# Another order for the mixer's tasks on four engines of one core, in a two-layer Hyena, MLA and GLA encoder

## The chip, the cores and the metric

The kernel runs on one core of one Trainium2 chip. Its time is the device time of one launch, in microseconds. The engines, each with its own queue of instructions, are TensorE (PE), VectorE (DVE), ScalarE (ACT), GpSimd (POOL) and SyncE (SP), which here issues transfers only.

## What is computed

A two-layer encoder on 256 rows of 1024 numbers, all in float32. Each layer is a half-weighted gated FFN, a mixer and a second half-weighted FFN, each on RMS-normed input and added to x:

```python
def hybrid_layer(x, ...):
    x = x + 0.5 * swiglu_ffn(rms_norm(x, ffn1_norm), ...)
    proj = rms_norm(x, mix_norm) @ w_in          # split in ten parts
    y_hy = hyena_mixer(hy_in, ...)
    y_mla = mla_mixer(mla_cq, mla_ckv, mla_kr, ...)
    y_gla = gla_mixer(gla_q, gla_k, gla_v, gla_gf, gla_gb, gla_r, ...)
    x = x + jnp.concatenate([y_hy, y_mla, y_gla], axis=-1) @ w_out
    return x + 0.5 * swiglu_ffn(rms_norm(x, ffn2_norm), ...)
```

The mixer has three branches. **Hyena** convolves 768 columns with three taps, splits them in v, x1 and x2, and computes z = x1 * longconv(v), y = x2 * longconv(z), where a long convolution is a transform, a complex product with the filter's spectrum and an inverse transform; then an RMS norm. **MLA** is attention of four heads from normed low-rank latents (256 for queries, 128 for keys and values), with 64 rotated columns per head, softmax over 256 keys, an RMS norm. **GLA** is gated linear attention of four heads in both directions, with gates log_sigmoid(...)/16; an RMS norm per head, times silu(r).

## The kernel before

**Splitting.** A float32 matrix product is made of three passes of TensorE over operands split in a high and a low part (`passes`, L921 to L925): high by high, high by low, low by high. Weights come as 1 MB slots through a ring of three buffers. SP fetches slot n when DVE has made the low part of slot n - 3 (L250 to L256); ACT makes the high part (`hi`, L372, w_high) once TensorE has used slot n - 3; DVE the low part (`lo`, L606, w_low); TensorE then uses it and counts `s_used`. Slots go in a fixed order: 33 of an FFN, the mixer's 15 (S_G3, S_G2, S_G1, S_G4 of two slots each for w_in; S_UQN, S_UQR, S_UKV for the latents; S_WO to S_WO+3 for w_out), 33 of the second FFN from FFN2 on. `Fori` runs the layer's body twice.

**The order in the mixer** is written out by hand, one list of calls per engine, tied by semaphores ("marks"). An engine does its list strictly in order, so an instruction that waits holds all that follow it. The parts that matter here:

- *Gates.* TensorE L1146 makes the gate logits after S_G1; DVE adds the bias (L825); ACT does Abs, Exp, Ln (L533 to L535); DVE makes the level exponents (L830 to L832).
- *Short convolution.* ACT writes the centre tap (`conv_centre`, L454), DVE adds the other two (`taps`, L697, L699), TensorE transposes (`turn_conv`, L1097), ACT copies out (`natural`, L457).
- *Long convolution* o (0 or 1): TensorE transforms (`hy_dft`, L1057); ACT copies the odd half (`spectrum_odd`); DVE's `products` adds and subtracts (L749, L750), multiplies by the filter's spectrum (L759, L760), combines (L761, L762) and folds (L763, L764, mark h_y); TensorE inverts (`hy_inverse`, L1069); DVE multiplies by x1 or x2 (`gated`, L769). The Hyena norm is a square on ACT (L579), a small chain on POOL (`rstd`) and a scale on DVE (L874).
- *Queries and keys.* TensorE makes q without and with rotation (S_UQN, S_UQR), then the first keys, values, second keys (S_UKV, L1181 on). DVE multiplies the rotated part by cosine and sine (L851 to L853, mark a_qt), POOL adds (L349, mark a_qr; L344 is the same for the keys), TensorE transposes (L1198), ACT copies the result (QR). ACT copies also QN, KN and VM from PSUM.
- *GLA levels* b = 0 to 7: ACT's `level_exp` (L480, into silu_gate), DVE's `level_qk` (L706), TensorE's `level_scores` (L1050), DVE's `level_keep` (L716, a masked copy; mark g_la). POOL's `levels` (L319, four adds) prepares the exponents of the next level. Level scores use PSUM banks 0 to 3 one after the other, so level b + 1 on TensorE waits for the keep of level b.
- *Attention* in two halves of 128 rows: `scores` (L1075, L1076), `score_max` (L721), `probs` (L489), `turn_probs` (L1083), `probs_turned`, `attend` (L1090), `attended` (L730).
- *Output.* `turn_group` (L930) transposes the three branches' outputs in four groups, `turned_high` and `turned_low` (L614) split them, `project` multiplies by w_out in quarters; L1245 is the GLA output. Then `update` (L646) and the next norm (L940).

For the change's own places, the list of TensorE around the first inverse is:

```python
keys((0, 1))
for t in range(T):
    e.wait_ge(g_vr.sem, g_vr.at(l, t + 1))
    passes(PS[:, 5 + t, :], KVH..., WH[p][:, 1, :], WL[p][:, 1, :], True, True)
e.wait_ge(h_pr.sem, h_pr.at(l, 1))
keys((2, 3)).then_inc(s_used.sem, 1)
hy_inverse(l, 0, 0).then_inc(h_inv.sem, 1)
e.wait_ge(a_qr.sem, a_qr.at(l))
```

## Time and profile before

| | us |
|---|---|
| median of 3 runs (1086.48 to 1090.4) | 1088.77 |
| the profiled execution, whole | 1088.98 |
| its span in the profile | 1087.2 |
| TensorE busy in the span | 1035.0 |
| DVE, ACT, POOL busy | 607.5, 493.0, 104.5 |
| mixer of layer 1, first conv transposes to the next norm | 259.1 to 350.4 |
| mixer of layer 2, the same | 793.4 to 886.1 |

Times in the rows are counted from the start of the span. A row of the waits says which line waited for which, how long in all, how often, and the longest. A row of the timeline gives start and duration in us, engine, line, instruction, operands and shapes, how many were merged, and in brackets the idle time of the engine before it and what ended it. PEclk is the clock granted to TensorE as a share of 2.4 GHz. Ends of matmuls are modelled, so one can overlap the next by a few tenths of a microsecond.

### The profile page before, as it was taken

The numbers are of one execution on the slowest core, as the hardware profiler recorded it, in microseconds if no ns is written. First come the engines' busy times: TensorE is split into PE (matmuls) and PEld (weight loads), VectorE is DVE, ScalarE is ACT, GpSimd is POOL, SyncE is SP. The second block draws the span as 40 slices with busy tenths as digits, with TensorE's granted clock in tenths as the row PEclk, the third lists the DMA queues.
The fourth block names the chain that finished last, engine by engine and source line by source line (L and its number), as shares of the span: only waits on it lengthen the run. The fifth ranks groups of instructions, "written<-read, shape, count | busy, mean of one in ns | idle before, by whom it ended". The sixth has DMA issues, their size and how long they took to land.

```text
span 1087.2 us, 18043 instructions
## 1 busy us (share of the span) xinstructions
PE 1035.0 (95%) x7060; PEld 936.7 (86%) x7060; DVE 607.5 (56%) x650; ACT 493.0 (45%) x654; POOL 104.5 (10%) x159
## 2 busy tenths in 40 slices
PE   6999999998789999999999999999977999999996
PEld 6999999787468999999889999998865789999995
DVE  4644454756964645444565554457579455445544
ACT  6443344447444534444364344435565454433342
POOL 1000000331511000000010000005025110000000
PEclk9999999999889999999999999999997999999998
DMA  8554545245312455555445455544242026554551
GB/s 306 204 205 178 187 187 193 81 153 194 116 40 78 168 186 187 193 186 176 180 153 208 182 190 193 193 155 155 94 178 85 33 78 233 187 184 175 188 203 49
DMA packets 26117, 177.07 MB, mean 163 GB/s; under 512 B 3120, under 2 KB 3632, under 8 KB 5200
## 3 DMA queue, kind: packets, MB, share of 16 engines
q1 hardware_dynamic: 24912, 174.21, 44.0%
q0 software_dynamic: 720, 1.95, 0.7%
q8 instruction: 36, 0.59, 0.2%
q10 hardware_dynamic: 432, 0.18, 0.1%
q14 instruction: 17, 0.14, 0.0%
HBM read 175.63 MB, written 1.05 MB: 163 GB/s over the span
## 4 chain that ended last, share of the span: by engine, by line
issue 89%; POOL 9%; POOLq 0%; DMA 0%; DVE 0%; ACT 0%; DVEq 0%; SPq 0%
POOL mixer_scratch L319 4%; POOL mixer_scratch L340 1%; POOL mixer_scratch L339 1%; POOL statistics L296 1%; POOL statistics L306 0%; DMA x<-in_x_dram 0%; POOL x_normed L344 0%; POOLq L220 0%; POOL mixer_scratch L341 0%; POOL statistics L305 0%; POOL statistics L303 0%; DVE x_normed L913 0%; POOL x_normed L349 0%; POOL statistics L295 0%; POOL statistics L294 0%
## 5 line engine op out<-in xcount | busy, mean ns | idle before, releaser
L609 DVE TENSOR_TENSOR w_low<-w_raw,w_high 128x2048 fp32r<-128x2048 f32 x163 | 375.4, 2306 | 234.1 <-ACT w_high L378 234.1
L923 PE MATMUL psum<-xT_high,w_high 128*128 128x256 f32 x1536 | 437.0, 285 | 4.0 <-DVE xT_low L614 3.4
L925 PE MATMUL psum<-xT_high,w_low 128*128 128x256 f32 x1536 | 434.6, 283 | 0.0
L924 PE MATMUL psum<-xT_low,w_high 128*128 128x256 f32 x1536 | 434.6, 283 | 0.0
L378 ACT ACTIVATE w_high<-w_raw 128x2048 fp32r<-128x2048 f32 x163 | 311.2, 1915 | 119.6 <-PE psum L925 117.0
L923 PEld LDWEIGHTS psum<-xT_high,w_high 128*128 128x128 f32 x1536 | 294.6, 192 | 8.0 <-DVE xT_low L614 4.1
L924 PEld LDWEIGHTS psum<-xT_low,w_high 128*128 128x128 f32 x1536 | 294.6, 192 | 1.9 <-issue 0.5
L925 PEld LDWEIGHTS psum<-xT_high,w_low 128*128 128x128 f32 x1536 | 294.6, 192 | 0.0
L407 ACT ACTIVATE silu_gate<-psum 128x256 f32<-128x256 f32 x88 | 33.8, 384 | 273.0 <-PE psum L925 272.9
L923 PE MATMUL psum<-w_high,hT_high 128*128 128x512 f32 (+1 forms) x360 | 139.9, 389 | 0.0
L924 PE MATMUL psum<-w_low,hT_high 128*128 128x512 f32 (+1 forms) x360 | 139.7, 388 | 0.0
L925 PE MATMUL psum<-w_high,hT_low 128*128 128x512 f32 (+1 forms) x360 | 139.2, 387 | 0.0
L629 DVE TENSOR_TENSOR hidden<-silu_gate,psum 128x256 f32<-128x256 f32 x88 | 37.0, 421 | 123.4 <-ACT silu_gate L407 123.4
L925 PEld LDWEIGHTS psum<-w_high,hT_low 128*128 128x128 f32 x360 | 67.6, 188 | 14.1
L923 PEld LDWEIGHTS psum<-w_high,hT_high 128*128 128x128 f32 x360 | 67.8, 188 | 13.4 <-issue 0.8
L303 POOL TENSOR_TENSOR statistics<-statistics,constants 128x1 f32<-128x1 f32 x14 | 2.7, 190 | 789.6 <-ACT x_normed L385 789.6
L924 PEld LDWEIGHTS psum<-w_low,hT_high 128*128 128x128 f32 x360 | 67.8, 188 | 12.2
L923 PE MATMUL psum<-w_high,xT_high 128*128 128x512 f32 (+1 forms) x128 | 51.7, 404 | 0.0
L319 POOL TENSOR_TENSOR mixer_scratch<-mixer_scratch 128x128 f32<-128x128 f32 x56 | 41.5, 741 | 105.1 <-ACT silu_gate L480 101.8
L449 ACT ACTIVATE mixer_scratch<-psum 128x512 f32<-128x512 f32 (+4 forms) x52 | 29.0, 606 | 48.2 <-PE psum L1097 18.5
L924 PE MATMUL psum<-w_low,xT_high 128*128 128x512 f32 (+1 forms) x128 | 50.0, 391 | 0.0
L925 PE MATMUL psum<-w_high,xT_low 128*128 128x512 f32 (+1 forms) x128 | 49.9, 390 | 0.0
(166 smaller groups left out, 782.6 us busy)
## 6 DMA issues: line engine op xcount, KB each, us to landing
w_raw<-in_w_dram SPq DMA_DIRECT2D x163, 1024.0 KB, 4.8
...
```

Source lines behind the costliest of these rows:

```text
L296: e.tensor_tensor(b, b, cst[:, I_POW:I_POW + n], ALU.pow).then_inc(done.sem, 1)
L319: return e.tensor_tensor(to[:, :, side, :], to[:, :, side, :], o, ALU.add)
L339: link(l, e.tensor_tensor(HS[:, p, o * 256:(o + 1) * 256], a, b, ALU.add))
L340: link(l, e.tensor_tensor(HD[:, p, o * 256:(o + 1) * 256], a, b, ALU.subtract))
L378: e.activation(WH[p][:], raw[p][:], ACT.Copy).then_inc(s_hi.sem, 1)
L407: e.activation(sg[:, f, :], PS[:, 4 + 2 * pr + f, 0:SEQ], ACT.Silu).then_inc(s_silu.sem, 1)
L449: r = e.activation(dst, src, ACT.Copy, **kw)
L609: e.tensor_tensor(WL[p][:], raw[p][:], WH[p][:].bitcast(F32), ALU.subtract).then_inc(s_lo.sem, 1)
L629: e.tensor_tensor(hid[:, f, :], sg[:, f, :], PS[:, 4 + 2 * pr + f, SEQ:2 * SEQ], ALU.mult).then_inc(s_h.sem, 1)
L923: e.matmul(out, ah, bh, start=start, stop=False)
L924: e.matmul(out, ah, bl, start=False, stop=False)
L925: return e.matmul(out, al, bh, start=False, stop=stop)
```

## The change

No arithmetic changes; calls change their places in the lists, `products` is cut in `join`, `multiply`, `combine` and `fold`, and two marks are new: a_km is signalled by the first keys and a_vm by the values, so that ACT can copy them before all of S_UKV is used. Some waits move with the calls. By engine:

- POOL: levels(2) comes after the rotation add (L349) instead of before it; the Hyena `rstd` before levels 4 and 5.
- ACT: the high splits of S_G4 and S_G4+1 come earlier, those of S_WO+1 and S_WO+2 later; VG and RG are copied in two halves around `natural(3)` and the split of S_WO; the first keys' copy comes before the first levels; the level exponentials are spread out among the softmax and copies.
- DVE: S_G1+1 and S_G4+1 are split earlier, S_WO+1, S_WO+2 and S_WO+3 later; the first product is spread around the splits of S_UQR and S_UKV; the rotation of the queries and both products come before the levels 1 and 2.
- TensorE: the first transform comes before the rows of S_G4+1, the first inverse before the second keys, the second transform before the query transposes; heads of scores, levels and projection quarters are interleaved differently, and a quarter of the first projection group follows the GLA output.

The diff, with the indentation of the engines' bodies cut and no context lines:

```diff
@@ -202 +202 @@
-        a_kn, a_v = mark("k_copied", 2), mark("v_copied", 2)
+        a_km, a_vm, a_kn, a_v = mark("first_keys", 1), mark("values", 1), mark("k_copied", 2), mark("v_copied", 2)
@@ -347 +346,0 @@
-levels(l, 2)
@@ -349,0 +349 @@
+levels(l, 2)
@@ -350,0 +351 @@
+rstd(l, h_sq, 2, T_SH, T_RH, I_H, 2, h_r)
@@ -353 +353,0 @@
-rstd(l, h_sq, 2, T_SH, T_RH, I_H, 2, h_r)
@@ -515,0 +516,11 @@
+def values_out(t):
+    e.wait_ge(s_used.sem, used(l, S_G4 + 1))
+    copy(VG[:, t, :], PS[:, 5 + t, 0:256])
+    copy(RG[:, t, :], PS[:, 5 + t, 256:512], g_vr)
+def attended_squares(s):
+    e.wait_ge(a_oe.sem, a_oe.at(l, s + 1))
+    e.activation(TT[:, 2 * s:2 * s + 2, :].rearrange("p a b -> p (a b)"), xn[:, s, 256:768], ACT.Square,
+                 accum_out=st[:, T_SM + s:T_SM + s + 1]).then_inc(a_sq.sem, 1)
@@ -520,0 +532 @@
+hi(l, S_G4)
@@ -529,2 +541 @@
-natural(l, 1, 2, 4)
-hi(l, S_G4)
+hi(l, S_G4 + 1)
@@ -536 +546,0 @@
-hi(l, S_G4 + 1)
@@ -541,0 +552 @@
+natural(l, 1, 2, 4)
@@ -543 +554 @@
-natural(l, 3, 1, 4)
+spectrum_odd(l, 0, 1)
@@ -546,5 +556,0 @@
-e.wait_ge(s_used.sem, used(l, S_G4 + 1))
-for t in range(T):
-    copy(VG[:, t, :], PS[:, 5 + t, 0:256])
-    copy(RG[:, t, :], PS[:, 5 + t, 256:512], g_vr)
-spectrum_odd(l, 0, 1)
@@ -552 +558,2 @@
-level_exp(l, 1)
+values_out(0)
+natural(l, 3, 1, 4)
@@ -553,0 +561,4 @@
+values_out(1)
+e.wait_ge(a_km.sem, a_km.at(l))
+copy(KN[:, 0:2, :].rearrange("p a b -> p (a b)"), PS[:, 4, :], a_kn)
+level_exp(l, 1)
@@ -557,5 +568 @@
-level_exp(l, 2)
-hi(l, S_WO + 1)
-e.wait_ge(s_used.sem, used(l, S_UKV))
-copy(KN[:, 0:2, :].rearrange("p a b -> p (a b)"), PS[:, 4, :], a_kn)
-copy(KN[:, 2:4, :].rearrange("p a b -> p (a b)"), PS[:, 1, :], a_kn)
+e.wait_ge(a_vm.sem, a_vm.at(l))
@@ -564 +571 @@
-level_exp(l, 3)
+spectrum_odd(l, 1, 7)
@@ -568,2 +575,4 @@
-spectrum_odd(l, 1, 7)
-hi(l, S_WO + 2)
+hi(l, S_WO + 1)
+e.wait_ge(s_used.sem, used(l, S_UKV))
+copy(KN[:, 2:4, :].rearrange("p a b -> p (a b)"), PS[:, 1, :], a_kn)
+level_exp(l, 2)
@@ -572,5 +581,2 @@
-level_exp(l, 4)
-level_exp(l, 5)
-probs(l, 0)
-level_exp(l, 6)
-probs_turned(l, 0)
+hi(l, S_WO + 2)
+level_exp(l, 3)
@@ -580,2 +586,5 @@
-level_exp(l, 7)
-turned_high(l, 2, 0, Y_BANKS[0], Y_TILES[0], C_GO, by_parity)
+level_exp(l, 4)
+probs(l, 0)
+level_exp(l, 5)
+probs_turned(l, 0)
+level_exp(l, 6)
@@ -582,0 +592 @@
+turned_high(l, 2, 0, Y_BANKS[0], Y_TILES[0], C_GO, by_parity)
@@ -584,4 +594,3 @@
-for s in range(T):
-    e.wait_ge(a_oe.sem, a_oe.at(l, s + 1))
-    e.activation(TT[:, 2 * s:2 * s + 2, :].rearrange("p a b -> p (a b)"), xn[:, s, 256:768], ACT.Square,
-                 accum_out=st[:, T_SM + s:T_SM + s + 1]).then_inc(a_sq.sem, 1)
+level_exp(l, 7)
+attended_squares(0)
+attended_squares(1)
@@ -590,2 +599,2 @@
-for g in range(1, 3):
-    turned_high(l, 2, g, Y_BANKS[g], Y_TILES[g], C_GO)
+turned_high(l, 2, 1, Y_BANKS[1], Y_TILES[1], C_GO)
+turned_high(l, 2, 2, Y_BANKS[2], Y_TILES[2], C_GO)
@@ -741 +750 @@
-            def products(l, o, b):
+            def join(l, o, b):
@@ -751 +760,6 @@
-e.wait_ge(h_pr.sem, h_pr.at(l, o + 1))
+            def pairs(v):
+return v.rearrange("p (j c) n -> p j c n", c=2)
+            def multiply(l, o):
@@ -754,0 +769,11 @@
+e.wait_ge(h_pr.sem, h_pr.at(l, o + 1))
+e.tensor_tensor(pairs(Y), pairs(C), both(KA[:]), ALU.mult)
+link(l, e.tensor_tensor(pairs(TT), pairs(C), both(KI[:]), ALU.mult))
+            def combine(l):
+y, t = pairs(Y), pairs(TT)
+e.tensor_tensor(y[:, :, 0, :], y[:, :, 0, :], t[:, :, 1, :], ALU.subtract)
+link(l, e.tensor_tensor(y[:, :, 1, :], y[:, :, 1, :], t[:, :, 0, :], ALU.add))
+            def fold(l):
@@ -756,7 +780,0 @@
-def four(v):
-    return v.rearrange("p (j c) n -> p j c n", c=2)
-u, yy, tt = four(C), four(Y), four(TT)
-e.tensor_tensor(yy, u, both(KA[:]), ALU.mult)
-link(l, e.tensor_tensor(tt, u, both(KI[:]), ALU.mult))
-e.tensor_tensor(yy[:, :, 0, :], yy[:, :, 0, :], tt[:, :, 1, :], ALU.subtract)
-link(l, e.tensor_tensor(yy[:, :, 1, :], yy[:, :, 1, :], tt[:, :, 0, :], ALU.add))
@@ -767,0 +786,2 @@
+if o == 0:
+    e.wait_ge(c_nat.sem, c_nat.at(l, 3))
@@ -811,0 +832,2 @@
+lo(l, S_G1 + 1)
@@ -818,3 +839,0 @@
-e.wait_ge(q_hi.sem, q_hi.at(l, 2))
-e.scalar_tensor_tensor(out=KVL[:], in0=PS[:, 6, 0:SEQ], scalar=par[:, C_KVN:C_KVN + 1],
-                       in1=KVH[:].bitcast(F32), op0=ALU.mult, op1=ALU.subtract).then_inc(q_lo.sem, 1)
@@ -822 +841 @@
-lo(l, S_G1 + 1)
+e.memset(G[:, 2:4, :], 0.0)
@@ -828 +847,4 @@
-e.memset(G[:, 2:4, :], 0.0)
+e.wait_ge(q_hi.sem, q_hi.at(l, 2))
+e.scalar_tensor_tensor(out=KVL[:], in0=PS[:, 6, 0:SEQ], scalar=par[:, C_KVN:C_KVN + 1],
+                       in1=KVH[:].bitcast(F32), op0=ALU.mult, op1=ALU.subtract).then_inc(q_lo.sem, 1)
+lo(l, S_G4 + 1)
@@ -833 +854,0 @@
-lo(l, S_G4 + 1)
@@ -836,0 +858,2 @@
+join(l, 0, 0)
+multiply(l, 0)
@@ -840,3 +863,3 @@
-products(l, 0, 0)
-level_qk(l, 1)
-lo(l, S_WO)
+combine(l)
+fold(l)
@@ -854 +876,0 @@
-level_qk(l, 2)
@@ -856,4 +878,7 @@
-level_qk(l, 3)
-lo(l, S_WO + 1)
-e.wait_ge(a_qr.sem, a_qr.at(l))
-products(l, 1, 6)
+lo(l, S_WO)
+level_qk(l, 1)
+join(l, 1, 6)
+multiply(l, 1)
+combine(l)
+fold(l)
+level_qk(l, 2)
@@ -861 +886,2 @@
-level_qk(l, 4)
+gated(l, 1, 6)
+level_qk(l, 3)
@@ -864,7 +890 @@
-level_qk(l, 5)
-lo(l, S_WO + 2)
-level_keep(l, 2)
-gated(l, 1, 6)
-level_qk(l, 6)
-level_keep(l, 3)
-level_qk(l, 7)
+level_qk(l, 4)
@@ -876 +896,2 @@
-level_keep(l, 4)
+level_keep(l, 2)
+level_qk(l, 5)
@@ -878 +899 @@
-turned_low(l, 2, 0, Y_BANKS[0], Y_TILES[0], C_GO, by_parity)
+level_keep(l, 3)
@@ -879,0 +901,2 @@
+level_keep(l, 4)
+turned_low(l, 2, 0, Y_BANKS[0], Y_TILES[0], C_GO, by_parity)
@@ -880,0 +904 @@
+level_qk(l, 6)
@@ -881,0 +906 @@
+level_qk(l, 7)
@@ -887,0 +913 @@
+lo(l, S_WO + 1)
@@ -891,0 +918 @@
+lo(l, S_WO + 2)
@@ -899 +925,0 @@
-lo(l, S_WO + 3)
@@ -900,0 +927 @@
+lo(l, S_WO + 3)
@@ -1126 +1152,0 @@
-filter_dft(l, 1)
@@ -1129 +1154,0 @@
-e.wait_ge(q_kr.sem, q_kr.at(l))
@@ -1133,0 +1159,2 @@
+filter_dft(l, 1)
+e.wait_ge(q_kr.sem, q_kr.at(l))
@@ -1159 +1185,0 @@
-rows(l, 1, S_G4 + 1, 1, 512, (5, 6)).then_inc(s_used.sem, 1)
@@ -1161,0 +1188 @@
+rows(l, 1, S_G4 + 1, 1, 512, (5, 6)).then_inc(s_used.sem, 1)
@@ -1186 +1213 @@
-keys((0, 1))
+keys((0, 1)).then_inc(a_km.sem, 1)
@@ -1189,3 +1216,2 @@
-    passes(PS[:, 5 + t, :], KVH[:, t * P:(t + 1) * P], KVL[:, t * P:(t + 1) * P], WH[p][:, 1, :], WL[p][:, 1, :], True, True)
-e.wait_ge(h_pr.sem, h_pr.at(l, 1))
-keys((2, 3)).then_inc(s_used.sem, 1)
+    r = passes(PS[:, 5 + t, :], KVH[:, t * P:(t + 1) * P], KVL[:, t * P:(t + 1) * P], WH[p][:, 1, :], WL[p][:, 1, :], True, True)
+r.then_inc(a_vm.sem, 1)
@@ -1192,0 +1219,3 @@
+e.wait_ge(h_oc.sem, h_oc.at(l, 1))
+keys((2, 3)).then_inc(s_used.sem, 1)
+e.wait_ge(a_v.sem, a_v.at(l, 2))
@@ -1193,0 +1223,2 @@
+e.wait_ge(h_z.sem, h_z.at(l, 1))
+hy_dft(l, 1, 6)
@@ -1201,3 +1231,0 @@
-e.wait_ge(a_v.sem, a_v.at(l, 2))
-e.wait_ge(h_z.sem, h_z.at(l, 1))
-hy_dft(l, 1, 6)
@@ -1205 +1232,0 @@
-level_scores(l, -1)
@@ -1206,0 +1234,3 @@
+e.wait_ge(a_kn.sem, a_kn.at(l, 2))
+level_scores(l, -1)
+scores(l, 0, (2,))
@@ -1208 +1238,2 @@
-scores(l, 0, (2, 3)).then_inc(a_s.sem, 1)
+scores(l, 0, (3,)).then_inc(a_s.sem, 1)
+hy_inverse(l, 1, 6).then_inc(h_inv.sem, 1)
@@ -1210 +1241,2 @@
-hy_inverse(l, 1, 6, (0,))
+e.wait_ge(h_z.sem, h_z.at(l, 2))
+scores(l, 1, (0, 1, 2))
@@ -1212 +1243,0 @@
-hy_inverse(l, 1, 6, (1,)).then_inc(h_inv.sem, 1)
@@ -1213,0 +1245 @@
+scores(l, 1, (3,)).then_inc(a_s.sem, 1)
@@ -1215,5 +1247 @@
-e.wait_ge(h_z.sem, h_z.at(l, 2))
-scores(l, 1, (0, 1))
-level_scores(l, 4)
-scores(l, 1, (2, 3)).then_inc(a_s.sem, 1)
-e.wait_ge(a_pte.sem, a_pte.at(l, 1))
+attend(l, 0)
@@ -1222,2 +1250 @@
-attend(l, 0)
-level_scores(l, 5)
+level_scores(l, 4)
@@ -1224,0 +1252,2 @@
+level_scores(l, 5)
+attend(l, 1)
@@ -1229,2 +1257,0 @@
-attend(l, 1)
-project(l, 0, 0, 1)
@@ -1233 +1260 @@
-project(l, 0, 1, 0)
+project(l, 0, 0, 1)
@@ -1235 +1262 @@
-project(l, 0, 1, 1).then_inc(s_used.sem, 1)
+project(l, 0, 1, 0)
@@ -1247,0 +1275 @@
+project(l, 0, 1, 1).then_inc(s_used.sem, 1)
```

## Rows read from the trace of the kernel before

**Rows 1.** Page, part 1: busy time of each engine.
```profile
PE 1035.0 (95%) x7060; PEld 936.7 (86%) x7060; DVE 607.5 (56%) x650; ACT 493.0 (45%) x654; POOL 104.5 (10%) x159
```

**Rows 2.** Waits of TensorE, 251 to 351 us: total, times, longest.
```profile
PE psum L1069 <- DVE mixer_scratch L764: 3.4, 1, 3.4
PE psum L1050 <- DVE mixer_scratch L716: 3.0, 2, 2.0
PE psum L1097 <- DVE mixer_scratch L699: 2.7, 2, 1.7
PE psum L1198 <- POOL x_normed L349: 2.7, 1, 2.7
PE psum L1083 <- ACT mixer_scratch L489: 1.3, 1, 1.3
PE psum L930 <- DVE x_normed L874: 0.9, 1, 0.9
```

**Rows 3.** Windows, 275 to 310 us: PE, PEld, DVE, ACT, POOL busy, PEclk, DMA.
```profile
275.00:310.00 35.00, 25.86 (x156) 17.15 (x155) 30.81 (x34) 15.36 (x33) 15.65 (x22) 0.80 0.30 116
```

**Rows 4.** Timeline of TensorE: start, duration, line, shapes, count [wait before it].
```profile
244.38 1.13 PE L1146 MATMUL psum<-hidden,gate_weights 32*128 32x256 f32 x4
...
259.14 0.72 PE L1097 MATMUL psum<-constants,mixer_scratch 128*128 128x128 f32 x4 [1.74 <-DVE mixer_scratch L699]
...
268.46 0.47 PE L923 MATMUL psum<-hT_high,w_high 128*128 128x256 f32 x1
...
275.27 0.28 PE L923 MATMUL psum<-kvT_high,w_high 128*128 128x256 f32 x1
...
350.39 0.82 PE L940 MATMUL psum<-diag_rstd,x 128*128 128x128 f32 x5 [0.30 <-DVE diag_rstd L621]
...
793.43 0.72 PE L1097 MATMUL psum<-constants,mixer_scratch 128*128 128x128 f32 x4 [1.74 <-DVE mixer_scratch L699]
...
886.13 2.05 PE L940 MATMUL psum<-diag_rstd,x 128*128 128x128 f32 x16 [0.30 <-DVE diag_rstd L621]
```

**Rows 5.** Timeline of TensorE: eight 256-column passes, twice.
```profile
266.92 1.89 PE L1057 MATMUL psum<-mixer_scratch,dft 128*128 128x256 f32 x8
...
279.55 3.65 PE L1069 MATMUL psum<-mixer_scratch,inverse_dft 128*128 128x256 f32 x8 [3.40 <-DVE mixer_scratch L764]
```

**Rows 6.** Timeline of ACT: gate logarithm, copies of QR.
```profile
252.40 0.64 ACT L535 ACTIVATE mixer_scratch<-mixer_scratch 128x512 f32<-128x512 f32 x1
...
287.43 1.07 ACT L449 ACTIVATE mixer_scratch<-psum 64x512 f32<-64x512 f32 x2 [2.06 <-PE psum L1198]
```

**Rows 7.** Timeline of DVE: first taps; S_UKV's split; first and last operation of the second product.
```profile
257.08 0.48 DVE L697 SCALAR_TENSOR_TENSOR mixer_scratch<-psum,par,mixer_scratch 128x255 f32<-128x255 f32 x1
...
270.65 2.29 DVE L609 TENSOR_TENSOR w_low<-w_raw,w_high 128x2048 fp32r<-128x2048 f32 x1 [3.60 <-ACT w_high L378]
...
290.45 0.69 DVE L749 TENSOR_TENSOR mixer_scratch<-psum,mixer_scratch 128x512 f32<-128x512 f32 x1 [1.70 <-PE psum L1057]
...
296.52 0.90 DVE L764 TENSOR_TENSOR mixer_scratch<-mixer_scratch 128x512 f32<-128x512 f32 x1
```

**Rows 8.** Timeline of DVE and POOL: a split beside POOL's add; rotation adds, two levels.
```profile
227.35 2.29 DVE L609 TENSOR_TENSOR w_low<-w_raw,w_high 128x2048 fp32r<-128x2048 f32 x1
...
227.52 2.44 POOL L344 TENSOR_TENSOR x_normed<-mixer_scratch 128x128 f32<-128x128 f32 x1 [2.10 <-DVE mixer_scratch L809]
...
284.50 1.26 POOL L349 TENSOR_TENSOR x_normed<-mixer_scratch 128x512 f32<-128x512 f32 x1
...
285.73 4.31 POOL L319 TENSOR_TENSOR mixer_scratch<-mixer_scratch 128x128 f32<-128x128 f32 x4
...
300.02 1.86 POOL L319 TENSOR_TENSOR mixer_scratch<-mixer_scratch 128x128 f32<-128x128 f32 x4 [3.15 <-ACT silu_gate L480]
```

**Rows 9.** Page, parts 5 and 6: high splits on ACT; transfers of weights.
```profile
L378 ACT ACTIVATE w_high<-w_raw 128x2048 fp32r<-128x2048 f32 x163 | 311.2, 1915 | 119.6 <-PE psum L925 117.0
...
w_raw<-in_w_dram SPq DMA_DIRECT2D x163, 1024.0 KB, 4.8
```

More of the change, by code:

```diff
@@ L853, in _ @@
                 e.tensor_tensor(t2[:, :, :, 32:64], q[:, :, :, 0:32], rp(1, 32, 64), ALU.mult).then_inc(a_qt.sem, 1)
+                gated(l, 0, 0)
+                lo(l, S_WO)
[4 more added lines that the diff above has]
+                fold(l)
                 level_qk(l, 2)
-                gated(l, 0, 0)
+                level_keep(l, 0)
+                gated(l, 1, 6)
                 level_qk(l, 3)
-                lo(l, S_WO + 1)
-                e.wait_ge(a_qr.sem, a_qr.at(l))
-                products(l, 1, 6)
-                level_keep(l, 0)
-                level_qk(l, 4)
                 score_max(l, 0)
                 level_keep(l, 1)
-                level_qk(l, 5)
-                lo(l, S_WO + 2)
-                level_keep(l, 2)
-                gated(l, 1, 6)
-                level_qk(l, 6)
-                level_keep(l, 3)
-                level_qk(l, 7)
+                level_qk(l, 4)
                 e.wait_ge(h_r.sem, h_r.at(l))
@@ L875, in _ @@
                 r.then_inc(h_yy.sem, 1)
+                level_keep(l, 2)
+                level_qk(l, 5)
+                score_max(l, 1)
+                level_keep(l, 3)
+                attended(l, 0)
                 level_keep(l, 4)
-                score_max(l, 1)
                 turned_low(l, 2, 0, Y_BANKS[0], Y_TILES[0], C_GO, by_parity)
-                attended(l, 0)
                 level_keep(l, 5)
+                level_qk(l, 6)
                 attended(l, 1)
+                level_qk(l, 7)
                 level_keep(l, 6, 4)
```

16 lines of the change are left out of this document (8 added, 8 removed).

## The prediction

> **What bounds the kernel now.** I read the page first. TensorE is busy 1035.0 of 1087.2 us [rows 1], so only time in which it waits, or runs slowly, can be won. The waits of TensorE come next, over the two mixers, since all edits lie there. From the conv transposes to the next norm it waits 3.4 + 3.0 + 2.7 + 2.7 + 1.3 + 0.9 = 14.0 us in layer 1 [rows 2]; layer 2 repeats the six rows within 0.2 us, 14.1 us together. What ends each is a DVE or POOL instruction queued behind others: the taps before the conv transposes (two waits, 1.7 and 1.0), the last add of the first spectrum product (3.4), POOL's add for the rotated queries (2.7), the masked keep of a level (2.0 and 1.0), the softmax (1.3), the Hyena rescale (0.9).
>
> The view by windows gives the second loss. In 275 to 310 us the granted clock is 0.80 [rows 3]. Its levels are 2.4 and 1.2 GHz, so (1 - 0.80) / 0.5 x 35 = 14 us ran at the lower one. Only about 1.2 us of these were waits, so 12.8 us of work ran at half speed and lost half of it, 6.4 us. The timeline shows it on equal work: eight 256-column passes take 1.89 us at 266.92 and 3.65 us at 279.55, right behind the 3.4 us wait [rows 5]. Layer 2 goes from the first conv transpose to the norm in 886.13 - 793.43 = 92.70 us, layer 1 in 350.39 - 259.14 = 91.25 us [rows 4]; the waits are equal, so the 1.45 us are clock, and layer 2 loses 7.8. Both mixers lose 14.0 + 14.1 + 6.4 + 7.8 = **42.3 us** to waits and low clock. That is the pot.
>
> **The change, step by step.** Nearly no instruction is added: two semaphore increments and a few waits, all on signals that earlier waits of these queues have passed or soon will; I cost them at nothing. One inverse transform is no longer split in two, without new work. So what counts is which waits are left. I walk layer 1 with the old durations.
>
> *Gates and conv.* The logarithm ends at 253.04 because ACT does the 1.9 us high split of S_G4 ahead of it [rows 6, 9]. That split now comes before the latent copies, in time where ACT waited for TensorE; S_G4+1's takes its place but can start at 244.4, when S_G1's matmuls end and the gate's begin [rows 4], so it is done before the gate logits are, and the logarithm ends near 251.0. The low split of S_G4+1 leaves the space between it and the taps, and the taps start near 252.5 instead of 257.08 [rows 7]. They take 3.7 us and end at 256.3, before TensorE is through with S_G4's rows at 257.4. Both conv waits, 2.7 us, go. The forward transform is now ahead of S_G4+1's rows: it waits only for ACT's copy of V, some 0.2 us. This order costs TensorE nothing and gives ACT and DVE the transform 5.6 us earlier. S_G4+1's rows end at 266.9 - 2.7 + 0.2 + 1.5 = 265.9.
>
> *First product.* Before, DVE's low split of S_UKV stood idle 3.6 us for ACT and eight operations followed it until TensorE could go on at 279.55 [rows 5, 7]. Now join and multiply (4.0 us) run during S_G4+1's rows. The high split of S_UKV starts at 265.9, its low split ends at 270.2, and combine and fold need 2.6 us more: h_y at 272.85. The latent products, first keys and values took 275.27 - 268.46 = 6.8 us [rows 4], so TensorE gets there at 272.7; the values are not held up, since ACT copies VG and RG by 271.5. **Left: 0.2 us** instead of 3.4, and 0.15 for S_UKV itself, which shifts both.
>
> *Rotated queries.* The inverse takes 1.9 us at full clock, the second keys 0.7 (they ended 0.9 us after 275.27, at 276.15, where the 3.4 us wait began [rows 4, 5]; 0.2 of that is the tail), so TensorE arrives at the wait for a_qr at 275.5. ACT's second level exponential ends near 272.65, and POOL has levels(1) **ahead** of its rotation add: four adds, 1.86 to 4.3 us [rows 8], I take 2.8 since DVE then mostly reads PSUM. The add itself would start near 275.5, together with DVE's low split of S_WO. The bounds are 1.26 us [rows 8], the same add beside light DVE work, giving 276.9, and full exclusion until the split ends at 277.8, giving 279.0. I take the second, by the nearest row: POOL's other rotation add, a quarter of the elements, began at 227.52 beside such a split (227.35, 2.29 us) and took 2.44 us [rows 8]. **Left: 3.45 us**, where 2.7 stood. What would be late next is nothing: QN, VM and the gated product are done by 275.6.
>
> The Trainium skill, page "SBUF — State Buffer", section "SBUF: two separate sides", says that a VectorE operation with two SBUF inputs and a GpSimd operation that reads SBUF exclude each other, whoever starts first holding the port for the whole instruction. By that rule the wait is 3.45 us if the split starts first and 1.4 us if the add does; the row of 2.44 us agrees with the rule for the first order.
>
> *Second product.* The transform now precedes the query transposes, so DVE's join can start before QR is copied. The new gap is the copy of QR, 1.07 us [rows 6], between transposes and scores: **1.1 us**. The heads' scores cover most of the 7.0 us from join to fold (290.45 to 297.42, [rows 7]); TensorE has 7.5 us of scores and levels until it asks for the second inverse. The two keep waits, 3.0 us, go: heads or the inverse stand between one level's scores and the next while DVE does the keep, and two low splits (S_WO+1 and S_WO+2, 2.3 us each [rows 7, 8]) have left this stretch of DVE, which was busy 30.8 of 35 us [rows 3]. The split of S_WO+1 is wanted only for the second projection group, 25 us later.
>
> *Softmax and tail.* Hyena's rescale, now ahead of the third keep, is done near 297 and wanted near 302, so 0.9 goes. The second softmax comes after levels 5 and 6 on ACT: I find 0.65 us before the transposed probabilities and 0.55 before attend(1), against 1.3. The last quarter of the first projection moves behind the GLA output matmuls and covers the head norm; 1.6 us of work that had no wait to fill is moved, nothing more. The weight transfers follow their low splits: S_WO+1's split releases FFN2's first megabyte 25 us later than before, near 314, and a transfer lands 4.8 us after issue [rows 9], by 319, against a use near 326. Cover holds; if it went, each microsecond of lateness would be TensorE's.
>
> *Sum.* Waits left per layer: 0.2 + 0.15 + 0.2 + 3.45 + 1.1 + 0.65 + 0.55, with 0.2 for the wait on the second gated product, are 6.5 us. The clock: the 3.45 us wait looks like the 3.4 us wait that a fall followed, so I put in one fall per layer, at the cost read there, 3.65 - 1.89 = 1.76 us [rows 5]; the small waits behind it I take as too short. Together 8.26 a layer, 16.5 in both. Gain 42.3 - 16.5 = **25.8 us**. The profiled execution took 1088.98 us in all (1087.2 of span), 0.2 above the median 1088.77; 1088.98 - 25.8 = **1063.2 us**.
>
> **The rivals.**
> *The add is early and the clock holds.* If levels(1) ends ahead of the split, the wait is 1.4 and no fall follows: 2 x (2.05 + 1.76) = 7.6 us better, 1055.6. For it: the 1.26 us row [rows 8], and POOL only just misses. Against: the 2.44 us row, and the 4.31 us row of four level adds.
> *The levels stay the bound.* DVE remains nearly full from 278 to 308, and products and POOL's adds lengthen one another (in the second product the last add took 0.90, the first 0.69, [rows 7]; levels 4.31 us against 1.86, [rows 8]). Then the 3.0 us of keep waits stay, the softmax waits double (1.2), and one more clock fall comes: 5.9 a layer, 11.8 in both, 1075.0.
> *The clock stays down (slower than before).* The 3.45 us wait, then 1.1 for QR, then handshakes of a level each could keep the engine at 1.2 GHz from 279 on. TensorE has some 24 us of full-clock work up to attend(1) near 307, so this adds 24 - 1.8 = 22 a layer: 1063.2 + 44 = 1107. It decides against the change once more than 12.9 + 1.8 us of work per layer run at half clock. For it: the clock fell twice running in 300 to 307 in the old kernel. Against: each fall of the trace ended while work continued.
> *Nothing comes of it.* The moved splits make FFN2's first weights late and the FFN gives the gain back, within 0.3% (3.3 us, about what a measurement of this kernel can tell from no change). It would need lateness of 7 us before it costs anything.
>
> **How the numbers follow.** Forecast 0.66, early add 0.14, levels bound 0.14, clock down 0.03, nothing 0.03. The range goes from the early add to the levels bound, 1056 to 1075 us; that leaves out under 2 in 10, counting mixtures of missed small waits. Faster 0.94, same 0.03, slower 0.03.
>
> **What would show it.** No TensorE wait on the taps line; the first inverse waits under 1 us; a wait of 1.4 to 3.5 us on POOL's rotation add, now ahead of the forward transform of the second convolution, its add lasting over 2 us; a granted clock over 0.9 in the middle of the mixer; the next norm at 338 instead of 350.4. Wrong would be: keep waits still at 3 us, a new wait on w_low in the projection, or a clock of 0.8 or less from 279 to 310.

## The result, and the profile after

The changed kernel takes **1053.91 us** (median of 4 runs, 1053.77 to 1060.01), the old one 1088.84 beside it; the ratio is 0.9692 [0.9658, 0.9726]. The forecast was 1063.2 with a range of 1056 to 1075: the direction and the pot were right, the time fell 2.1 us below the range.

The profiled execution is the long one, 1060.01 us (span 1058.3). Its busy times [rows 1]:

```profile
PE 1027.3 (97%) x7060; PEld 931.1 (88%) x7060; DVE 608.7 (58%) x650; ACT 492.5 (47%) x654; POOL 105.6 (10%) x159
```

The same work is done; TensorE's busy time is shorter because less of it ran at the lower clock. In the changed kernel lines are 9 to 31 higher: `hy_dft` is L1084, `hy_inverse` L1096, `level_scores` L1077, the transposes of the conv L1124, the scores L1102, the taps L708. The waits of TensorE, 240 to 345 us (line that waited, line it waited for, total, times, longest), against [rows 2]:

```profile
PE psum L1102 <- ACT mixer_scratch L449: 1.2, 1, 1.2
PE psum L967 <- DVE diag_rstd L630: 0.8, 2, 0.5
PE psum L1077 <- DVE mixer_scratch L725: 0.5, 1, 0.5
PE psum L1096 <- DVE mixer_scratch L782: 0.5, 1, 0.5
PE psum L1084 <- POOL x_normed L348: 0.5, 1, 0.5
PE psum L950 <- DVE xT_low L623: 0.5, 1, 0.5
PE psum L957 <- DVE x_normed L925: 0.2, 1, 0.2
PE psum L1084 <- ACT mixer_scratch L449: 0.2, 1, 0.2
```

L967 and L950 belong to the norm behind the mixer and were there before. What is left in the mixer is 1.2 + 0.5 + 0.5 + 0.5 + 0.2 + 0.2 = **3.1 us**, in layer 2 as in layer 1, where 14 stood and 6.5 were forecast. Of the six old waits the conv, the softmax and the Hyena rescale are gone; the first product has kept 0.5 us, the keep 0.5, the rotated queries 0.5. New is the copy of QR, 1.2.

The timeline of TensorE, layer 1 (start, duration, ..., the wait before it in brackets), shows the walk step by step [rows 4, 5]:

```profile
257.17 1.11 PE L1124 MATMUL psum<-constants,mixer_scratch 128*128 128x128 f32 x8
258.49 1.99 PE L1084 MATMUL psum<-mixer_scratch,dft 128*128 128x256 f32 x8 [0.21 <-ACT mixer_scratch L449]
...
273.25 1.99 PE L1096 MATMUL psum<-mixer_scratch,inverse_dft 128*128 128x256 f32 x8 [0.50 <-DVE mixer_scratch L782]
...
276.45 1.97 PE L1084 MATMUL psum<-mixer_scratch,dft 128*128 128x256 f32 x8 [0.50 <-POOL x_normed L348]
...
280.45 0.70 PE L1102 MATMUL psum<-mixer_scratch 128*128 128x256 f32 x2 [1.16 <-ACT mixer_scratch L449]
...
284.61 1.22 PE L1102 MATMUL psum<-mixer_scratch 128*128 128x256 f32 x2
...
290.38 3.78 PE L1096 MATMUL psum<-mixer_scratch,inverse_dft 128*128 128x256 f32 x8
...
339.53 2.05 PE L967 MATMUL psum<-diag_rstd,x 128*128 128x128 f32 x16 [0.30 <-DVE diag_rstd L630]
```

One conv stage with no wait, 0.21 for the transform, the first inverse at 273.25 (forecast: h_y at 272.85), then 0.50 for a_qr where 3.45 were forecast. From about 282.4 on the same pair of score products takes 1.22 us instead of 0.70, and the second inverse 3.78 instead of 1.99: the clock is down. The view by windows, whose eighth column is PEclk, shows that only layer 1 of this execution has that [rows 3]:

```profile
275.00:310.00 35.00, 32.81 (x229) 22.23 (x227) 26.89 (x33) 17.62 (x41) 13.05 (x25) 0.80 0.08 31
...
810.00:845.00 35.00, 34.34 (x278) 26.63 (x278) 27.77 (x37) 19.43 (x48) 14.08 (x26) 1.00 0.14 49
```

A later profile of the same kernel (e16; four of its six executions took 1053.6 to 1054.2 us) caught an execution without the fall; its next norm and its windows:

```profile
333.41 2.05 PE L967 MATMUL psum<-diag_rstd,x 128*128 128x128 f32 x16 [0.30 <-DVE diag_rstd L630]
```
```profile
275.00:310.00 35.00, 32.69 (x280) 23.16 (x279) 32.23 (x40) 20.60 (x48) 14.09 (x28) 1.00 0.10 31
810.00:845.00 35.00, 34.25 (x272) 28.15 (x272) 27.16 (x35) 18.54 (x39) 9.83 (x16) 1.00 0.19 63
```

The waits are the same, and the norm comes 339.53 - 333.41 = 6.1 us earlier. That is what this one fall costs, and all of the difference between 1060 and 1054.

**Where the 34.9 us came from.** Every execution has a mean granted clock c and a span S; at two levels, (1 - c) x S is what the lower one cost, if TensorE works in that time (to 0.5 us, as c has three digits). The old kernel's executions have c of 0.974 to 0.986, 15 to 29 us lost; without that they would take 1069.4 to 1074.4. The changed kernel's usual ones have 0.997 to 0.998, 2 to 3 us lost, and would take 1050.4 to 1052.0. So some 20 us come from waits (the waits' view says 28.1 - 6.2 = 21.9) and some 15 from the clock. The two are not independent, as many falls come behind waits (last section). And the changed kernel's own 2 to 3 us cost nothing: they lie behind TensorE's last matmul, as the window of e16 from there to the end shows:

```profile
1043.50:1051.80 8.30, 0.00 (x0) 0.00 (x0) 4.08 (x7) 1.14 (x4) 1.11 (x4) 0.75 0.34 126
```

The profiles of the old kernel, e2, e3, e5, e6, e9 and e13 have 4 to 6.5 us at the lower clock there too, which makes each time without its loss 2 to 3 us too short, in all kernels alike. Below, "without the clock's loss" is this number, an estimate of which only the differences are used.

### The profile page after: what moved, and what is told of

Same layout as the page of the kernel before. It is cut to its first block, busy times and chain, and to the rows that moved or that the text cites. A ratio compares the mean times of both kernels' runs of the same rounds, so it can differ in the third digit from the quotient of the medians.

```text
span 1058.3 us, 18037 instructions
## 1 busy us (share of the span) xinstructions
PE 1027.3 (97%) x7060; PEld 931.1 (88%) x7060; DVE 608.7 (58%) x650; ACT 492.5 (47%) x654; POOL 105.6 (10%) x159
## 4 chain that ended last, share of the span: by engine, by line
issue 89%; POOL 9%; POOLq 1%; DMA 0%; DVE 0%; ACT 0%; DVEq 0%; SPq 0%
POOL mixer_scratch L319 4%; POOL mixer_scratch L340 1%; POOL mixer_scratch L339 1%; POOL statistics L296 1%; POOL statistics L294 1%; POOL statistics L306 1%; DMA x<-in_x_dram 0%; POOL x_normed L344 0%; POOLq L220 0%; POOL mixer_scratch L341 0%; POOL x_normed L348 0%; POOL statistics L305 0%; POOL statistics L303 0%; DVE x_normed L940 0%; POOL statistics L295 0%
## 5 line engine op out<-in xcount | busy, mean ns | idle before, releaser
L950 PE MATMUL psum<-xT_high,w_high 128*128 128x256 f32 x1536 | 437.0, 285 | 4.7 <-DVE xT_low L623 4.1
L950 PEld LDWEIGHTS psum<-xT_high,w_high 128*128 128x128 f32 x1536 | 294.6, 192 | 8.8 <-DVE xT_low L623 4.9
L950 PE MATMUL psum<-w_high,hT_high 128*128 128x512 f32 (+1 forms) x360 | 139.9, 389 | 0.0
L950 PEld LDWEIGHTS psum<-w_high,hT_high 128*128 128x128 f32 x360 | 67.8, 188 | 13.4 <-issue 0.8
L950 PE MATMUL psum<-w_high,xT_high 128*128 128x512 f32 (+1 forms) x128 | 51.1, 399 | 0.0
L319 POOL TENSOR_TENSOR mixer_scratch<-mixer_scratch 128x128 f32<-128x128 f32 x56 | 38.8, 692 | 95.2 <-ACT silu_gate L480 91.9
L411 ACT ACTIVATE hT_high<-hidden 128x256 fp32r<-128x256 f32 x88 | 35.7, 406 | 21.4 <-DVE hidden L638 21.4
```

Of the source, the lines that this page charges most:

```text
L319: return e.tensor_tensor(to[:, :, side, :], to[:, :, side, :], o, ALU.add)
L411: e.activation(HHB[pr][:, f, :], hid[:, f, :], ACT.Copy).then_inc(s_hh.sem, 1)
L950: e.matmul(out, ah, bh, start=start, stop=False)
```

## The experiments

All are the changed kernel with one edit; no arithmetic of the result is left out. Each series had the old kernel beside it, at 1089.22 us (e1 to e4), 1091.28 (e5 to e8), 1091.59 (e9 to e12) and 1090.5 (e13 to e16).

**e1: who starts first.** DVE splits S_WO before the first gated product.

```diff
-gated(l, 0, 0)
 lo(l, S_WO)
+gated(l, 0, 0)
```

> The changed kernel with DVE's low split of S_WO put ahead of the first gated product, so that it starts about 1.6 us earlier, while POOL still works at levels(1). In the changed kernel POOL's adds won the race: the rotation add ended at 276.4 us and TensorE waited 0.5 us. Theory (the step of my sum had the exclusion right and the order wrong): with the split first, POOL's remaining level adds and the rotation add come after 276.7 us and a_qr near 278.5 to 279.5, so TensorE waits 2.5 to 3.5 us in each layer: 1058 to 1060 us if the clock holds, up to 1064 if a fall follows each wait. Rival (POOL and DVE don't exclude each other here, the short wait is simply what the adds take): only the gated product is 2.2 us later and TensorE waits for that, about 0.8 to 1.3 us a layer more, 1056 us, and the rotation add still takes under 1.4 us and ends before 277.

1060.65 us (1059.32 to 1065.94), ratio 0.9728 [0.9707, 0.9748]. DVE and POOL on the timeline:

```profile
274.32 2.42 DVE L618 TENSOR_TENSOR w_low<-w_raw,w_high 128x2048 fp32r<-128x2048 f32 x1
276.66 0.68 DVE L789 TENSOR_TENSOR mixer_scratch<-psum,mixer_scratch 128x512 f32<-128x512 f32 x1
```
```profile
272.70 4.30 POOL L319 TENSOR_TENSOR mixer_scratch<-mixer_scratch 128x128 f32<-128x128 f32 x4 [1.44 <-ACT silu_gate L480]
276.96 1.26 POOL L348 TENSOR_TENSOR x_normed<-mixer_scratch 128x512 f32<-128x512 f32 x1
```

In the changed kernel as it is, the same three stood so:

```profile
275.99 2.52 DVE L618 TENSOR_TENSOR w_low<-w_raw,w_high 128x2048 fp32r<-128x2048 f32 x1
```
```profile
272.75 2.37 POOL L319 TENSOR_TENSOR mixer_scratch<-mixer_scratch 128x128 f32<-128x128 f32 x4 [1.44 <-ACT silu_gate L480]
275.08 1.28 POOL L348 TENSOR_TENSOR x_normed<-mixer_scratch 128x512 f32<-128x512 f32 x1
```

The wait of TensorE, 240 to 345 us:

```profile
PE psum L1084 <- POOL x_normed L348: 2.4, 1, 2.4
```

With the split 1.7 us earlier, the four adds for level 1 take 4.30 us instead of 2.37, so the rotation add comes 1.9 us later and TensorE waits 2.4 us for it in both layers, instead of 0.5. The mechanism is the theory's; its wait came out a tenth short, its time 0.6 us long. Without the clock's loss e1 takes 1054.7 us, 3.4 more than the changed kernel's 1051.3, and twice 1.9 us of wait is 3.8.

**e2, e3: the predicted state, made on purpose.** One or three more adds of 128x512 on POOL, into memory that is free then, ahead of the rotation add.

```diff
 e.wait_ge(a_qt.sem, a_qt.at(l))
+e.tensor_tensor(PE_[:, 0:2, :], dft[:], dft[:], ALU.add)
 e.tensor_tensor(xn[:, :, 768:1024], TT[:, 0:2, :], TT[:, 2:4, :], ALU.add).then_inc(a_qr.sem, 1)
```

> The changed kernel with one more add of the same size (128x512, 1.26 us) on POOL ahead of the rotation add, into memory that is free then. Theory of exclusion: the extra add holds the port until 276.4, DVE's low split then comes in between, and the rotation add ends near 279.9 instead of 276.4: 3.5 us more a layer for 1.26 us of work, 1061 us with the clock held. Rival (no exclusion): 1.26 us more a layer, 1056.4 us. The clock: if a wait of some 4 us brings a fall, the profile shows a granted clock of 0.50 behind it and the time is another 3.5 us longer.

e2: 1065.07 us (1061.88 to 1069.51), 0.9767 [0.9726, 0.9807]. POOL and DVE (lines one higher; L348 is the extra add, L349 the rotation):

```profile
274.96 1.04 POOL L348 TENSOR_TENSOR mixer_scratch<-dft 128x512 f32<-128x512 f32 x1
275.96 3.31 POOL L349 TENSOR_TENSOR x_normed<-mixer_scratch 128x512 f32<-128x512 f32 x1
```
```profile
275.87 2.28 DVE L619 TENSOR_TENSOR w_low<-w_raw,w_high 128x2048 fp32r<-128x2048 f32 x1
```

This is the case of the forecast to the tenth: the split starts 0.09 us before the add, which lasts 3.31 us instead of 1.26, and TensorE waits

```profile
PE psum L1085 <- POOL x_normed L349: 3.5, 1, 3.5
```

in both layers, for 1.04 us of work added. The order and the wait are the forecast's. The time comes in two groups, 1061.88 and 1061.94 us, and 1068.21 and 1069.51; the profiled execution, one of the second group, has a long fall of the clock in layer 1 besides (last section). So the forecast's 1063.2 is 1.3 us above the first group, and that the median comes near it is in part chance. The changed kernel misses that state by 0.9 us: its add starts at 275.08, the split at 275.99.

> The changed kernel with three more adds of 1.26 us on POOL ahead of the rotation add. Both on exclusion and without it TensorE waits 3.8 to 6 us more a layer than in the changed kernel: 1061.5 to 1066 us if the clock holds. What this run is for is the clock: my sum put a fall of 1.76 us behind a wait of 3.45 us. If that rule holds, both layers show a granted clock of 0.50 behind the wait in every execution, and the time is at least 3.5 us above 2 x the added wait. If the clock doesn't follow single waits, some executions show no fall and the time is the added wait alone.

e3: 1071.65 us (1068.52 to 1076.48), 0.9823 [0.9791, 0.9855], a wait of 6.0 us in both layers. Without the clock's loss the three kernels take 1051.3, 1057.9 and 1060.3 us for waits of 0.5, 3.5 and 6.0: the first step costs 6.6 us where twice the wait is 6.0, the second 2.4 where it is 5.0. Half of what is missing in the second, 1.3 of 2.6 us, is time counted twice: in e3 the clock is down for the last 1.7 and 1.0 us of the two waits (granted 0.86 and 0.92 over the 6.0 us). The rest is not explained. On the clock, which this run was for, the forecast's rule of one fall per layer held: in the profile each wait has its fall, of 6.8 us, all four executions lost at least 8.5 us to the clock where the kernel's end accounts for 2 to 3, and the shortest time is 3.6 us above 1053.9 + 2 x 5.5. In e2 it held in the profile (last section), but the two shorter executions leave 1061.9 - 1053.9 - 6.1 = 1.9 us for the clock, about one fall and not two.

**e4: the first keys' own signal.** ACT waits for all of S_UKV, as it did before, to copy the first keys.

```diff
-e.wait_ge(a_km.sem, a_km.at(l))
+e.wait_ge(s_used.sem, used(l, S_UKV))
```

> The changed kernel with the new signal of the first keys not used: ACT waits for the whole use of S_UKV before it copies the first keys (the copies of QN and VM and the second level's exponential stand behind it). Theory: ACT then stands until the second keys are done near 275.9 us instead of 271.2, VM is copied by 279.5, and TensorE waits for it ahead of the second transform, some 3 us a layer more: 1060 us, 1062 or more with clock falls. Rival (the signals are worth nothing, the order does it all): under 1 us, within 1053.5 to 1055.

1070.17 us (1068.45 to 1076.07), 0.9833 [0.9796, 0.987]. The time without the clock's loss, 1060.3, is as expected, but by luck: the way is another. TensorE waits 5.9 us in both layers for the rotated queries, 5.4 more, where 3 more were expected, and for the values, since the second level exponential stands behind that copy on ACT, and POOL has that level's adds ahead of the rotation. TensorE's wait, then ACT (the exponential started at 271.89 in the changed kernel), then POOL:

```profile
PE psum L1084 <- POOL x_normed L348: 5.9, 1, 5.9
```
```profile
275.80 0.60 ACT L449 ACTIVATE mixer_scratch<-psum 128x512 f32<-128x512 f32 x1 [4.65 <-PE psum L952]
276.29 0.77 ACT L480 ACTIVATE silu_gate<-mixer_scratch 128x256 f32<-128x256 f32 x2
```
```profile
277.14 3.18 POOL L319 TENSOR_TENSOR mixer_scratch<-mixer_scratch 128x128 f32<-128x128 f32 x4 [6.01 <-ACT silu_gate L480]
280.28 1.26 POOL L348 TENSOR_TENSOR x_normed<-mixer_scratch 128x512 f32<-128x512 f32 x1
```

One increment of a semaphore, costed at nothing in the forecast, is worth 16 us in this order, 9 of them without the clock's loss. The forecast had the exponential at 272.65 by that signal, without pricing its loss.

**e5, e6, e7: the conv and the first product put back**, alone and together (the diff is shortened, and its comments are put in here): the order of the splits of S_G4, S_G4+1, S_G1+1 and `natural(1)` as in the old kernel (e5); join and multiply behind the split of S_UKV (e6).

```diff
@@ e5, ACT and DVE @@
-hi(l, S_G4)                    # ahead of the latent copies
+hi(l, S_G4)                    # behind them
-hi(l, S_G4 + 1)                # ahead of Abs, Exp, Ln
+hi(l, S_G4 + 1)                # behind them
-lo(l, S_G4 + 1)                # ahead of the gates
+lo(l, S_G4 + 1)                # between gates and taps
@@ e6, DVE @@
-join(l, 0, 0)
-multiply(l, 0)
 lo(l, S_UQR)
 level_qk(l, 0)
 lo(l, S_UKV)
+join(l, 0, 0)
+multiply(l, 0)
 combine(l)
```

> The changed kernel with the old places of the splits of S_G4 and S_G4+1 on ACT and of S_G4+1 on DVE (the taps start near 257 again). Theory: the two waits on the taps come back (1.7 and 1.0 us in each layer), all later work moves by 2.7 us and nothing hides it: 5.4 us without clock, 1059.3 us where the changed kernel has 1053.9, 1 to 6 us more if the clock falls. Rival (these waits only moved the wait for the first inverse): under 2 us, 1056 at most.

> The changed kernel with the first product in one piece behind the split of S_UKV again (join and multiply no longer run during S_G4+1's rows). Theory: h_y comes 4.0 us later, TensorE waits some 4.3 us for the first inverse instead of 0.5; the rotation multiplies shift with it, so POOL's add is 3 to 4 us later as well, but inside the same shift: 3.5 to 4.5 us a layer, 1061 to 1063 us with the clock held and up to 1070 with falls as in the old kernel. Rival (POOL's chain is the bound, and the product's early part is hidden anyway): under 2 us.

> The changed kernel with both the split order of the gates and the one-piece product undone. What is left of the change then is the order of the query chain, the levels, the softmax and the tail. Theory: the two costs add (2.7 + 4 us a layer), and the clock falls as in the old kernel: 1067 us with the clock held, 1070 to 1080 as it falls; so the rest of the change is worth 10 to 20 us against the old kernel's 1089. Rival: the two parts overlap (an early product needs early taps), then this kernel is no slower than the one with the product alone undone by more than 2 us.

TensorE's waits in layer 1, first of e5, then of e6:

```profile
PE psum L1124 <- DVE mixer_scratch L708: 2.7, 2, 1.7
```
```profile
PE psum L1096 <- DVE mixer_scratch L782: 4.6, 1, 4.6
```

e5: 1061.97 us (1061.06 to 1062.4), 0.9713 [0.966, 0.9765]: the 2.7 us of [rows 2] are back; without the clock's loss 1056.8, 5.5 more, as 2 x 2.7 says. e6: 1065.9 us (1064.34 to 1069.08), 0.9761 [0.9706, 0.9816]: 4.6 us for the first inverse instead of 0.5, and the 0.5 us for a_qr gone, 3.6 a layer on balance; without the clock's loss 1058.3, 7.0 more. e7: 1072.48 us (1070.29 to 1074.31), 0.9805 [0.9751, 0.9859], both waits; 1063.3, 12.0 more, and the parts make 5.5 + 7.0 = 12.5. So the two account for 12 of the 20 us of waits, the rest of the change for 8.

**e8: two weight splits back among the levels.** lo(S_WO+1) ahead of the first keep, lo(S_WO+2) behind level_qk(4).

```diff
 level_qk(l, 2)
+lo(l, S_WO + 1)
 level_keep(l, 0)
@@
 level_qk(l, 4)
+lo(l, S_WO + 2)
```

> The changed kernel with DVE's low splits of S_WO+1 and S_WO+2 back among the levels (behind the third level_qk, and behind the second keep). Theory: each holds DVE for 2.3 us where TensorE needs the keeps and the softmax maximum, so keep and score waits of 1.5 to 4.5 us a layer come back: 1057 to 1063 us. Rival (DVE has room there: it stood 4.5 us idle before the second gated product): within 1 us of 1053.9.

1064.0 us (1060.67 to 1066.32), 0.9736 [0.9678, 0.9794]. The keep wait is back, in layer 1 and, below it, in layer 2 (765 to 870 us):

```profile
PE psum L1077 <- DVE mixer_scratch L725: 2.1, 2, 1.6
```
```profile
PE psum L1077 <- DVE mixer_scratch L725: 3.7, 4, 1.6
```

That is 1.6 and 3.2 us more than the 0.5 of the changed kernel. In layer 1 the clock was down for 10.2 us behind the first of these waits, and the later keeps were in time for the slower TensorE; in layer 2 it stayed up. So the waits and the clock can't be told apart here by the mean clock: without its loss the four executions take 1052.5 to 1056.4 us, the more the less they lost to it, 1.2 to 5.1 more than the changed kernel. By the same number the clock takes 4 to 14 us of each execution instead of 2 to 3. In all, by the medians, the two moved splits are worth 10 us.

**e9 to e12: the small waits that are left.** e9 is the changed kernel again; in e10 POOL's rotation add comes before levels(1), in e11 the query transposes before the transform, so that ACT copies QR beside it; e12 has both.

```diff
@@ e10, POOL @@
-levels(l, 1)
 e.wait_ge(a_qt.sem, a_qt.at(l))
 e.tensor_tensor(xn[:, :, 768:1024], TT[:, 0:2, :], TT[:, 2:4, :], ALU.add).then_inc(a_qr.sem, 1)
+levels(l, 1)
@@ e11, TensorE @@
-e.wait_ge(h_z.sem, h_z.at(l, 1))
-hy_dft(l, 1, 6)
 ...
 r.then_inc(a_qtr.sem, 1)
+e.wait_ge(h_z.sem, h_z.at(l, 1))
+hy_dft(l, 1, 6)
```

> The changed kernel once more, beside the next three on one chip: 1053.5 to 1054.5 us, or about 1060 in executions in which the clock falls for some 13 us.

> The changed kernel with POOL's rotation add ahead of levels(1). Theory (the order on POOL is what is left of the wait): the add starts when the rotation multiplies are done (274.45 us) and ends at 275.8, before TensorE gets there at 275.95: the 0.5 us goes, 1.0 us in both layers, 1052.9 us. Levels(1) then runs into the split of S_WO and ends near 281, still ahead of the third level's exponential at 282.6. Rival: that exponential, and with it the levels, becomes late, and nothing is won or 1 us lost.

> The changed kernel with the query transposes ahead of the second forward transform again (and ACT's copy of QR ahead of its copy of the odd half). Theory: the copy of QR (1.07 us) hides under the transform, the wait of 1.2 us goes; DVE's join started only at 279.0, behind the split of S_WO and level_qk(1), and the transform ends at 279.3 then, so the product moves by 0.2 to 0.4 us, which the scores cover: 2 x 1.1 = 2.2 us less, 1051.7 us. Rival (the product chain is the bound, so the wait comes back at the second inverse or the keeps): 1053 to 1054 us.

> The changed kernel with both edits: the add ahead of levels(1), the query transposes ahead of the second transform. Theory: both waits go, 3.2 us in all, 1050.7 us. Rival: the levels' or the product's chain takes the place of what was won, 1052 to 1054 us.

e9: 1053.9 us (1053.54 to 1058.61), 0.9658 [0.9628, 0.9687]. e10: 1056.21 (1053.85 to 1063.48), 0.9684 [0.9648, 0.972]; a_qr is early, but TensorE then waits 0.3 us for the gated product, and three of the six executions lost 7 to 13 us to the clock; without its loss e10 takes 1051.3, as the changed kernel does. e11: 1055.15 (1053.45 to 1056.92), 0.9657 [0.9629, 0.9685]: the wait on QR is gone, and the second inverse now waits 1.1 us for the fold, which it had not. e12: 1056.76 (1054.95 to 1056.89), 0.9669 [0.9642, 0.9697], on TensorE's timeline:

```profile
286.72 3.68 PE L1096 MATMUL psum<-mixer_scratch,inverse_dft 128*128 128x256 f32 x8 [1.64 <-DVE mixer_scratch L782]
```

The wait of 1.16 us at 280 has become one of 1.64 us at 285, with the inverse behind it at the lower clock in this layer (3.68 us for 1.99); in layer 2 the same wait is followed by an inverse of 1.99 us. The intervals overlap e9's; nothing is won by either, alone or together.

**e13 to e16: the copy of QR in two halves.** The turned queries are signalled per two heads, ACT copies each half on its signal, and the first two heads' scores wait for the first half only. e14 adds e10's edit; e15 has level_qk(1) ahead of the first gated product, in 0.9 us in which DVE waits; e16 is the changed kernel.

```diff
-r.then_inc(a_qtr.sem, 1)
-e.wait_ge(a_qre.sem, a_qre.at(l, 2))
+    if h % 2:
+        r.then_inc(a_qtr.sem, 1)
+e.wait_ge(a_qre.sem, a_qre.at(l, 1))
 scores(l, 0, (0, 1))
+e.wait_ge(a_qre.sem, a_qre.at(l, 2))
```

> The changed kernel with a finer signal: the turned queries are signalled and copied in two halves of two heads, and the scores of the first two heads wait for the first half alone. The wait on the copy is 1.16 us, of which one copy (about 0.5 us) and half the transposes (about 0.4 us) are avoidable. Theory (the copy's term of the sum is a real bound, and nothing else stands just behind it): the wait falls to 0.3 us, 0.8 to 0.9 us a layer are won, 1052.2 us (1051.5 to 1053.0). Rival (the second product is next, as in the kernels that swapped transposes and transform): TensorE reaches the second inverse 0.85 us earlier and waits there; 1053.9 us.

> The same halves, and POOL's rotation add ahead of levels(1), which makes both small waits that are left near 280 us short. Theory (small waits pay one for one): 0.9 + 0.2 us a layer, 1051.8 us. Rival (the second inverse is the next bound; the earlier TensorE comes, the longer it waits there, and a clock fall may follow): 1054 to 1057 us, with a wait of over 0.5 us on the fold.

> The same halves, and DVE's level_qk(1) ahead of the first gated product, in the 0.9 us in which DVE waits for the first inverse, so that the second product starts and ends 0.7 us earlier. Theory (if the second inverse has become the bound): its wait goes, 1051.8 to 1052.5 us, better than the halves alone by the wait seen there. Rival (level_qk(1) reads SBUF twice on DVE and collides with POOL's adds for level 1, so that the rotation add starts later, beside or behind the split of S_WO): the wait for the rotated queries grows from 0.5 to between 1.0 and 3.5 us, 1055 to 1059 us.

> The changed kernel itself once more, beside the three on the same chip. Theory: 1053.9 us as twice before, in most executions 4 to 6 us at the lower clock. It is the measure for differences of under 2 us, and for how often an execution of it has over 14 us at the lower clock (2 of 11 so far).

e13: **1053.33 us**, 0.9652 [0.9624, 0.968]; its sixth execution took 2566.84 us, as one of the old kernel beside it took 2019.22, both at a full granted clock, from a cause that the record doesn't show; the other five lie between 1053.22 and 1053.39. e14: 1053.5 (1053.33 to 1053.77); e15: 1053.41 (1053.3 to 1053.67); e16: 1053.95 (1053.59 to 1059.88), 0.9677 [0.9646, 0.9708]. Among TensorE's waits of e13, 240 to 345 us:

```profile
PE psum L1077 <- ACT mixer_scratch L449: 0.3, 1, 0.3
PE psum L1077 <- DVE mixer_scratch L725: 0.3, 1, 0.3
...
PE psum L1102 <- ACT mixer_scratch L449: 0.2, 1, 0.2
PE psum L1110 <- ACT mixer_scratch L489: 0.2, 1, 0.2
```

The copy's wait fell from 1.16 to 0.24 us as expected, and 0.6 us of 1.8 were won. The lead is lost in small pieces: TensorE is 0.85 us ahead of e16 behind the copy (279.61 for 280.46), then come 0.27 for the copy ahead of the level scores (L1077) and 0.21 at the softmax (L1110), while the keep's wait falls from 0.52 to 0.25; between 301 and 321 us another 0.2 go with no wait in the trace. At the next norm e13 stands at

```profile
333.17 2.05 PE L967 MATMUL psum<-diag_rstd,x 128*128 128x128 f32 x16 [0.30 <-DVE diag_rstd L630]
```

0.24 us ahead of e16's 333.41. Neither theory nor rival is right: the path is held by several chains at once, each some tenths behind the next. e15's edit did collide with POOL's adds, but cost 0.3 us at a_qr, not 0.5 to 3.0. e14 gained 0.3 us more up to 282 and gave it back in a wait of 0.42 us at the second inverse. The three are the fastest versions measured, by some 0.05%.

## Why the prediction was wrong, point by point

- **The pot (42.3 us)** held: the kernel won 34.9 of it.
- **Gates and conv, 2.7 us:** right in time and mechanism (taps at 252.58 for 252.5, transform wait 0.21 for 0.2; e5).
- **First product:** right; 0.50 us left for 0.2, and nothing for S_UKV's 0.15 (e6).
- **Rotated queries: the step that failed.** It took 2.8 us for POOL's four adds of levels(1) and so had the rotation add start near 275.5 *together with* the split, and gave the split precedence by the row of 2.44 us. The adds took 2.37 us; the add started at 275.08, the split 0.9 us later, and it was the split that was lengthened (2.52 for 2.29). 0.50 us were left, not 3.45: 5.9 us in two layers. The exclusion and the wait of the chosen order were right, as e2 shows (3.5 us); the choice was made by the row of 2.44 us, in which the split had started first, where only the start times decide, and the walk had these to half a microsecond (275.08 and 275.99 for 275.5). e1 and e2 turn the order round, one from either side, and bring the wait. The add's end, 276.36, lies below the forecast's lower bound of 276.9. The rival of the early add had the order and the held clock right (its wait of 1.4 was 0.5, its 1055.6 was 1053.9), at a chance of 0.14.
- **The clock, 2 x 1.76 us:** set for a 3.45 us wait that did not come, so it went with the step before. For such a wait it was about right: in e2's profile the clock fell behind it in both layers, and layer 2's transform took 3.54 us for 1.97, 1.6 more. The changed kernel's usual execution has no fall in its mixers. The fall of its profiled execution is another, which the forecast did not have: no wait over 1.2 us before it, from 282.4 to about 296, and 6.1 us.
- **Softmax, 2 x 1.20 us:** none was left in the changed kernel, and 0.2 in e13 and e2. I did not test the cover by itself.
- **Against it:** the keep kept 0.5 us where I had none, and L957 waits 0.2. The copy of QR was 1.16 for 1.1.
- **Sum:** 5.9 + 3.5 + 2.4 + 0.7 (gated product, S_UKV) - 1.0 (keep) - 0.6 (first inverse) - 0.4 (L957) - 0.1 (QR) = 10.4 against 1063.2 - 1053.9 = 9.3. About 1 us stays unplaced; e13 shows that waits of some tenths do not add one for one, so no closer sum is to be had from them.
- **The rivals:** the levels no longer bound (e8 shows that the moved splits are why); the clock did not stay down for good in any run, even behind waits of 6.0 us; FFN2's weights were in time (no wait on w_low in either layer).

The Trainium skill, page "SBUF — State Buffer", section "SBUF: two separate sides", has whoever starts first hold the shared port for the whole instruction. The forecast gave by it 1.4 us of wait if the add starts first and 3.45 if the split does. The traces agree with the second (3.5 us, e2) and with the order; with the add ahead by 0.9 us the wait is 0.5, as the add was then nearly through.
